# Eight weight slots from the middle of the output projections on, and the high part of x ahead of its square

## The chip, the core and the metric

The kernel runs as one program on one core of a Trainium2 chip. What is measured is the device time of one execution in microseconds (us). In the text, "PE" is TensorE, "ACT" ScalarE, "DVE" VectorE, "POOL" GpSimd and "SP" SyncE.

## The reference, cut to what matters

512 tokens of width 1024 pass through a gMLP layer, a squared-ReLU MLP, a banded attention layer, a second squared-ReLU MLP, a SwiGLU half step, a mixer with two branches (sparse attention and retention), a second SwiGLU half step and a gated addition. Every product is a float32 matrix product, and in front of most of them stands an RMS norm of the running stream h:

```python
def rms_norm(x, g):
    y = xf * lax.rsqrt(jnp.mean(xf * xf, axis=-1, keepdims=True) + RMS_EPS)
    return (y * g).astype(x.dtype)

h = h + rms_norm(m, g[1])                                      # m: output projection of the layer
f = sq_relu_mlp(rms_norm(h, g[2]), w_up[layer], w_down[layer])
h = h + rms_norm(f, g[3])
...
h = h + merged @ w_out[i]
h = h + 0.5 * swiglu(rms_norm_2(h, ffn2_norm[i]), ...)
```

## The kernel before, in words

**Split products.** PE multiplies in fp32r. Weights and activations are each split into a high and a low part, and a product is three passes per tile: high weights with high x, high weights with low x, low weights with high x. Activations are feature-major: eight tiles of 128 features by 512 tokens. XH and XL hold the two parts of x, and HH and HL those of a hidden activation.

**Units.** All weights form one list of 411 units of 128 x 1024, in the order of use. FIRST names where each product begins: gmlp_out at 16, ffn_a0 at 24, att_v at 88, att_out at 112, ffn_a1 at 120, ffn_b1 at 184, mix_heads at 252, merge at 287, mix_out at 319, ffn_b2 at 327, ple at 395. SP loads unit u into one of four raw buffers once unit u - 4 is split. Splitting is two instructions: high (a copy to fp32r) and low (raw minus high). For the units of POOL_RANGES both are done by POOL (L362, L365). For the others ACT makes the high part (split_high, L865) and DVE the low part (split_low, L1206), eight units ahead of the product whose output they are taking (AHEAD). The first such unit behind a POOL range waits until POOL has finished the range: DVE by `dve.wait_ge(weights_split, SLOTS + u)`, ACT by its counterpart on high_split.

**Slots.** Split weights lie in four slots (WH, WL) or, inside the ranges of WIDE, in eight (WH2, WL2 and, where these are taken, WHA and WLA). A slot may be filled when the unit before it in that slot is done (`units_done`). With four slots that is unit u - 4, with eight it is u - 8. WIDE begins one or two groups behind each output projection.

**PE's products.** `product` takes one unit, and a plain unit is 24 matmuls. `together` takes three or four units side by side, feature tile by feature tile, so that it can begin while later tiles of x are still being made. `token_major_half` does the same with x as the stationary operand. Before the last tile they call `stat`, which sums the squares over the partitions and must wait for the last of them; afterwards `spread` lays 1/rms out over the partitions. The bank of PSUM for a unit is u mod 4, but a few units (SPARE) use bank 7.

**A norm.** x is scaled by 1/rms only after the product, so the parts of x need the gain alone. For each tile t, DVE updates H, ACT writes the square to T (`square`) and the high part to XH, and DVE adds the square to SS (`add_square`) and writes XL (`pre_tile`). `post_and_pre` is the norm behind an MLP or projection whose own output was normed, `half_step` that behind a SwiGLU. `branch` evacuates an output projection tile by tile: DVE copies the bank, ACT squares it, DVE adds the square, and then DVE's split_low for eight units ahead stands in the same queue.

Of the kernel before, what the change touches and what calls it, by code (L numbers as in the profile page):

```python
# [151 lines left out]
def program(nc, xT, weights, gains, cols, lng, lnb, bs, wsT, rel, pos, ident_d, decay, pT, out):  # L152
    with ExitStack() as ctx:
# [32 lines left out]
        WHA = at("WHA", 188, [P, 3, UNIT], F32R)  # L186
# [156 lines left out]
        def _(pool):  # L343
# [3 lines left out]
            def split_units(u, n, step=0):  # L347

                for v in range(u, u + n):
# [40 lines left out]
        def _(pe):  # L390
# [4 lines left out]
            ss, ri = Count(ss_ready), Count(ri_ready)  # L395
# [40 lines left out]
            def together(*units, before_last=None):  # L436


# [31 lines left out]
            def token_major_half(ready=None, before_last=None):  # L470


                first = split.n
                for q in range(4):
# [4 lines left out]
                    for kk in range(2):  # L479
# [3 lines left out]
                        if ready is not None:  # L483
                            pe.wait_ge(ready.sem, ready.now(back=DT - 1 - k))
                        w = slice(kk * SEQ, kk * SEQ + SEQ)
                        for j in range(TT):
                            tok = slice(j * P, j * P + P)
                            for n, (x, wt) in enumerate(((XH, high), (XL, high), (XH, low))):
                                last = nc.tensor.matmul(PS[:, (first + j) % SLOTS, :], x[:, k, tok],  # L489
                                                        wt[:, w], start=(k == 0 and n == 0),  # L490
                                                        stop=(k == DT - 1 and n == 2))
                    last.then_inc(units_done, 1)

            def products_token_major(ready=None, before_last=None):

                if ready is not None:
                    token_major_half(ready, before_last)
# [30 lines left out]
            def ffn(tiles, gated):  # L528
# [3 lines left out]
                def group(size, first=False):  # L532
                    if first:
                        together(*[(DT, XH, XL, xr)] * SLOTS, before_last=stat)
                        spread(5)
# [73 lines left out]
            products_token_major(xr, stat)  # L609
# [14 lines left out]

            xr.next(DT)
# [4 lines left out]
            products_token_major(xr, stat)  # L630
# [19 lines left out]
            def out_high(n, k):  # L650

                w = slice(k * P, k * P + P)
                nc.tensor.matmul(PS[:, out_bank(n), :], WH[:, n % SLOTS, w], OH[:, k, :], start=(k == 0), stop=False)
                return nc.tensor.matmul(PS[:, out_bank(n), :], WL[:, n % SLOTS, w], OH[:, k, :], start=False,
                                        stop=False)

            def out_low(n, k):
# [3 lines left out]
                                        WH[:, n % SLOTS, w], OL[:, :, w], start=False, stop=(k == DT - 1))  # L661
# [85 lines left out]

            xr.next(DT)
            ffn(FFN_A, False)
            stat_and_spread()  # L750

            xr.next(DT)
# [3 lines left out]
            together(*[(DT, XH, XL, xr)] * 3, before_last=stat)  # L756
# [64 lines left out]

            xr.next(DT)
# [14 lines left out]
        def _(act):  # L837
# [983 lines left out]
```

## Time and profile before

| | |
|---|---|
| device time, median of 3 runs | 2685.99 us (2682.25 to 2686.25) |
| the profiled execution's own time | 2688.23 us |
| its span in the trace | 2686.4 us |
| granted clock of PE, mean of the span | 0.944 |
| PE busy | 2489.5 us (93%) |
| DVE, ACT, POOL busy | 1364.6, 760.4, 610.2 us |

Times inside the trace count from the start of the span. The granted clock is 1.0 when PE runs at 2.4 GHz and 0.5 at 1.2 GHz. A busy share is an average over stages, and what ends last in each stage is read from the waits and the timeline.

### The profile page before, as it was taken

The numbers are of one execution on the slowest core, as the hardware profiler recorded it, in microseconds if no ns is written. First come the engines' busy times: TensorE is split into PE (matmuls) and PEld (weight loads), VectorE is DVE, ScalarE is ACT, GpSimd is POOL, SyncE is SP. The second block draws the span as 40 slices with busy tenths as digits, with TensorE's granted clock in tenths as the row PEclk, the third lists the DMA queues.
The fourth block names the chain that finished last, engine by engine and source line by source line (L and its number), as shares of the span: only waits on it lengthen the run. The fifth ranks groups of instructions, "written<-read, shape, count | busy, mean of one in ns | idle before, by whom it ended". The sixth has DMA issues, their size and how long they took to land.

```text
span 2686.4 us, 29675 instructions
## 1 busy us (share of the span) xinstructions
PE 2489.5 (93%) x10924; PEld 1980.5 (74%) x10924; DVE 1364.6 (51%) x1947; ACT 760.4 (28%) x1200; POOL 610.2 (23%) x283
## 2 busy tenths in 40 slices
PE   6878999989996999998999997978899997999997
PEld 5666888877665788887888885664478885888886
DVE  4546434463663643445564456796344344544465
ACT  2114323331432432233322233302322111322232
POOL 6650000025335000000000005551037875000000
PEclk9888999989998999998999998985599998999999
DMA  4222333322223233331332322120012332433321
GB/s 166 73 78 68 110 97 99 94 63 77 78 63 94 63 102 102 94 99 55 118 101 87 92 81 63 55 71 24 16 40 78 94 94 79 117 97 92 93 77 59
DMA packets 64823, 221.79 MB, mean 83 GB/s; under 512 B 7504, under 2 KB 9680, under 8 KB 64592
## 3 DMA queue, kind: packets, MB, share of 16 engines
q1 hardware_dynamic: 59184, 208.17, 26.2%
q10 hardware_dynamic: 5536, 12.19, 1.4%
q8 instruction: 72, 1.18, 0.2%
q14 instruction: 31, 0.25, 0.0%
HBM read 218.23 MB, written 2.10 MB: 82 GB/s over the span
## 4 chain that ended last, share of the span: by engine, by line
PE 80%; DVE 10%; POOL 4%; ACT 3%; issue 2%; DMA 0%; POOLq 0%; ACTq 0%; DVEq 0%
PE PS L420 23%; PE PS L422 22%; PE PS L421 22%; PE PS L489 3%; POOL WH L362 2%; POOL WL L365 2%; PE PS L563 1%; PE PS L584 1%; DVE WL L1206 1%; PE PS L774 1%; PE PS L690 1%; PE PS L711 1%; PE PS L700 1%; DVE MK L1574 1%; PE PS L573 1%
## 5 line engine op out<-in xcount | busy, mean ns | idle before, releaser
L420 PE MATMUL PS<-XH,WH 128*128 128x512 f32 x1792 | 714.6, 399 | 40.2 <-DVE T L1425 12.5
L421 PE MATMUL PS<-XL,WH 128*128 128x512 f32 x1792 | 703.7, 393 | 0.0
L422 PE MATMUL PS<-XH,WL 128*128 128x512 f32 x1784 | 700.4, 393 | 0.0
L362 POOL TENSOR_TENSOR WH<-RAW,ONES 128x1024 fp32r<-128x1024 f32 (+1 forms) x136 | 266.9, 1963 | 1654.8 <-PE PS L422 1530.3
L1206 DVE TENSOR_TENSOR WL<-RAW,WH 128x1024 fp32r<-128x1024 f32 (+2 forms) x272 | 322.4, 1185 | 248.4 <-ACT WH L865 192.2
L420 PEld LDWEIGHTS PS<-XH,WH 128*128 128x128 f32 x1792 | 340.8, 190 | 130.7 <-issue 33.6
L422 PEld LDWEIGHTS PS<-XH,WL 128*128 128x128 f32 x1784 | 338.5, 190 | 72.0
L420 PE MATMUL PS<-HH,WH 128*128 128x512 f32 x992 | 389.0, 392 | 2.6 <-DVE HL L1278 2.6
L421 PEld LDWEIGHTS PS<-XL,WH 128*128 128x128 f32 x1792 | 340.6, 190 | 68.2
L422 PE MATMUL PS<-HH,WL 128*128 128x512 f32 x992 | 386.3, 389 | 0.0
L421 PE MATMUL PS<-HL,WH 128*128 128x512 f32 x992 | 386.1, 389 | 0.0
L865 ACT ACTIVATE WH<-RAW 128x1024 fp32r<-128x1024 f32 (+2 forms) x272 | 276.8, 1018 | 349.5 <-DVE M L1309 202.4
L365 POOL TENSOR_TENSOR WL<-RAW,WH 128x1024 fp32r<-128x1024 f32 (+1 forms) x132 | 322.5, 2443 | 10.4
L420 PEld LDWEIGHTS PS<-HH,WH 128*128 128x128 f32 x992 | 186.2, 188 | 50.0 <-issue 9.1
L422 PEld LDWEIGHTS PS<-HH,WL 128*128 128x128 f32 x992 | 186.2, 188 | 38.9
L421 PEld LDWEIGHTS PS<-HL,WH 128*128 128x128 f32 x992 | 186.3, 188 | 37.9
L1278 DVE TENSOR_TENSOR HL<-T,HH 128x512 fp32r<-128x512 f32 x108 | 74.8, 692 | 127.2 <-ACT HH L928 92.7
L489 PE MATMUL PS<-WH,XH 128*128 128x512 f32 x192 | 82.3, 428 | 46.4 <-DVE XL L1226 22.4
L1218 DVE TENSOR_TENSOR SS<-SS,T 128x512 f32<-128x512 f32 x91 | 82.8, 910 | 24.5 <-ACT T L871 24.5
L925 ACT ACTIVATE T<-T 128x512 f32<-128x512 f32 x64 | 40.5, 632 | 184.9 <-DVE T L1285 184.9
L1309 DVE TENSOR_TENSOR M<-PS,M 128x512 f32<-128x512 f32 x48 | 33.1, 690 | 107.2 <-PE PS L422 106.8
L871 ACT ACTIVATE T<-H 128x512 f32<-128x512 f32 x72 | 45.4, 631 | 141.5 <-DVE H L1255 48.4
(208 smaller groups left out, 2467.6 us busy)
## 6 DMA issues: line engine op xcount, KB each, us to landing
RAW<-in_weights SPq DMA_DIRECT2D x379, 512.0 KB, 3.5
RAW<-in_weights SPq DMA_DIRECT2D x16, 384.0 KB, 3.2
H<-in_xT ACTq DMA_DIRECT2D x8, 256.0 KB, 8.2
BIAS<-in_rel ACTq DMA_DIRECT2D x8, 256.0 KB, 3.5
RAW<-in_weights SPq DMA_DIRECT2D x8, 256.0 KB, 2.7
out<-R ACTq DMA_DIRECT2D x8, 256.0 KB, 2.2
BIAS<-in_rel ACTq DMA_DIRECT2D x8, 224.0 KB, 3.9
DECAY<-in_decay ACTq DMA_DIRECT2D x1, 1024.0 KB, 4.9
```

Source lines behind the costliest of these rows:

```text
L362: nc.gpsimd.tensor_tensor(high[:, 0:w], raw, ONES[:, 0:1].to_broadcast([P, w]), ALU.mult).then_inc(high_split, 1)
L365: nc.gpsimd.tensor_tensor(low[:, 0:w], raw, high[:, 0:w].bitcast(F32), ALU.subtract).then_inc(weights_split, 1)
L420: nc.tensor.matmul(PS[:, bank_, :], high[:, w], xh[:, k, :], start=(k == 0), stop=False)
L421: nc.tensor.matmul(PS[:, bank_, :], high[:, w], xl[:, k, :], start=False, stop=False)
L422: return nc.tensor.matmul(PS[:, bank_, :], low[:, w], xh[:, k, :], start=False, stop=stop)
L489: last = nc.tensor.matmul(PS[:, (first + j) % SLOTS, :], x[:, k, tok], wt[:, w], start=(k == 0 and n == 0), stop=(k == DT - 1 and n == 2))
L865: S.activation(weights_of(u)[0][:, 0:w], RAW[:, slot, 0:w], ACT.Copy).then_inc(high_split, 1)
L871: S.activation(T[:, sq.n % 2, :], src, ACT.Square).then_inc(sq_ready, 1)
L925: S.activation(T[:, 1, :], T[:, 0, :], ACT.Square).then_inc(act_self, 1)
L1206: V.tensor_tensor(low[:, 0:w], RAW[:, slot, 0:w], high[:, 0:w].bitcast(F32), ALU.subtract).then_inc(weights_split, 1)
L1218: V.tensor_tensor(SS[:], SS[:], T[:, slot, :], ALU.add).then_inc(ss_ready, 1)
L1278: V.tensor_tensor(HL[:, f, :], T[:, src, :], HH[:, f, :].bitcast(F32), ALU.subtract).then_inc(h_ready, 1)
```

## The change

Two independent edits are made.

First, WIDE begins four units earlier: at 20, 116 and 323, the middle of the three output projections. POOL's splits of these units wait for other conditions (all low parts of x made, all scores read, all units before mix_out done) and not for the unit four places back. Free memory for the slots is taken from other places (WHX, WLX), and WHA goes away. The third POOL range ends at 331 instead of 335, so ACT and DVE split units 331 to 334.

Second, in the norms ACT writes the high part before the square, DVE writes XL before it adds the square (`low_part`, then `square_and_rest`), and in `post_and_pre` and `half_step` the low part of tile t - 1 stands between the two instructions that update H of tile t. In the first product of a norm PE waits for the high part alone (xh_ready), runs the two passes that read XH, then waits for XL and runs the third pass. This form is used for the first product of the first norm, of ffn_a0, att_v, ffn_a1, ffn_b1, mix_heads and ffn_b2. The first products of gmlp_out, mix_out and ple stay as they were.

```diff
-POOL_RANGES = ((0, 28), (92, 124), (256, 335))
+POOL_RANGES = ((0, 28), (92, 124), (256, 331))
-WIDE = ((24, 92, 20), (120, 256, 116), (331, UNITS, 328))
+WIDE = ((20, 92, 16), (116, 256, 112), (323, UNITS, 319))
...
-        WHA = at("WHA", 188, [P, 3, UNIT], F32R)
+        WHX = [at(f"WHX{n}", kb, [P, UNIT], F32R) for n, kb in enumerate((72, 76, 88, 92))]
+        WLX = [at(f"WLX{n}", kb, [P, UNIT], F32R) for n, kb in enumerate((188, 92, 192, 196))]
...
-            high = WHA[:, k - SLOTS, :] if 331 < u < 335 else WH2[:, k - SLOTS, :]
-            low = WLA[:, k - SLOTS, :] if 120 <= u < 124 else WL2[:, k - SLOTS, :]
+            high = WHX[k - SLOTS] if 323 <= u < 335 else WH2[:, k - SLOTS, :]
+            low = WLA[:, 2 * SLOTS - 1 - k, :] if 116 <= u < 120 else WLX[k - SLOTS] if 124 <= u < 128 else                 WL2[:, k - SLOTS, :]
...
-                    if v == 24:
+                    if v == FIRST["gmlp_out"] + SLOTS:
                         pool.wait_ge(x_ready, 2 * DT)
-                    elif v == 120:
+                    elif v == FIRST["att_out"] + SLOTS:
                         pool.wait_ge(x_done, 2 * DT * TT)
-                    elif v == 332:
+                    elif v == FIRST["mix_out"] + SLOTS:
                         pool.wait_ge(units_done, FIRST["mix_out"] + SLOTS)
...
+                    if high:
+                        pe.wait_ge(xh_ready, high(k))
+                        w = slice(k * P, k * P + P)
+                        for s, (tiles, xh, xl, ready) in enumerate(units):
+                            if k == 0:
+                                pe.wait_ge(weights_split, split.next())
+                                pe.wait_ge(evacuated, bank.next())
+                            for n, part in enumerate(weights_of(first + s)):
+                                nc.tensor.matmul(PS[:, (first + s) % SLOTS, :], part[:, w], xh[:, k, :],
+                                                 start=(k == 0 and n == 0), stop=False)
+                        pe.wait_ge(ready.sem, ready.now(back=tiles - 1 - k))
+                        for s, (tiles, xh, xl, ready) in enumerate(units):
+                            last = nc.tensor.matmul(PS[:, (first + s) % SLOTS, :], weights_of(first + s)[0][:, w],
+                                                    xl[:, k, :], start=False, stop=(k == tiles - 1))
+                            if k == tiles - 1:
+                                last.then_inc(units_done, 1)
+                        continue
...
             def pre_norm(gs, free, ready, evacuates=None):
+                act.wait_ge(units_done, free + SLOTS)
                 for t in range(DT):
                     act.wait_ge(ready.sem, ready.next())
-                    square(H[:, t, :])
-                    if t == 0:
-                        act.wait_ge(units_done, free + SLOTS)
-                    for g, dst in gs:
+                    for n, (g, dst) in enumerate(gs):
                         S.activation(dst[:, t, :], H[:, t, :], ACT.Copy, scale=gain(g, t)).then_inc(xh_ready, 1)
+                        if n == 0:
+                            square(H[:, t, :])
...
+            def low_part(t, g, dh, dl, ready):
+                dve.wait_ge(xh_ready, xh.next())
+                V.scalar_tensor_tensor(dl[:, t, :], H[:, t, :], gain(g, t), dh[:, t, :].bitcast(F32),
+                                       ALU.mult, ALU.subtract).then_inc(ready, 1)
+
+            def square_and_rest(t, gs):
+                add_square(t == 0)
+                for g in gs[1:]:
+                    low_part(t, *g)
+
             def pre_tile(t, gs):
-                add_square(t == 0)
-                for g, dh, dl, ready in gs:
-                    dve.wait_ge(xh_ready, xh.next())
-                    V.scalar_tensor_tensor(dl[:, t, :], H[:, t, :], gain(g, t), dh[:, t, :].bitcast(F32),
-                                           ALU.mult, ALU.subtract).then_inc(ready, 1)
+                low_part(t, *gs[0])
+                square_and_rest(t, gs)
```

## Rows read from the trace of the kernel before

**Rows 1.** The page: busy time, share of the span and instructions of each engine.

```profile
PE 2489.5 (93%) x10924; PEld 1980.5 (74%) x10924; DVE 1364.6 (51%) x1947; ACT 760.4 (28%) x1200; POOL 610.2 (23%) x283
```

**Rows 2.** The waits of PE: who waited for whom, total us, times, longest.

```profile
PE PS L509 <- DVE SS L1218: 45.1, 5, 19.0
...
PE PS L420 <- POOL WL L365: 9.8, 4, 4.1
PE PS L420 <- DVE T L1297: 9.1, 1, 9.1
```

**Rows 3.** Stretches A:B, their length, each engine's busy time, clock, DMA share, GB/s.

```profile
161.00:189.50 28.50, 28.50 (x127) 23.45 (x125) 9.02 (x10) 3.17 (x5) 27.81 (x13) 1.00 0.30 93
189.50:207.80 18.30, 0.20 (x1) 0.00 (x0) 7.55 (x9) 5.68 (x7) 7.85 (x4) 0.56 0.53 152
847.50:866.40 18.90, 0.00 (x0) 0.00 (x0) 7.53 (x9) 5.61 (x7) 8.52 (x5) 0.58 0.51 147
...
2226.00:2238.00 12.00, 3.69 (x12) 1.90 (x10) 12.00 (x6) 2.52 (x3) 11.74 (x5) 0.79 0.29 87
...
2269.40:2278.40 9.00, 0.08 (x1) 0.00 (x0) 1.81 (x2) 1.06 (x1) 6.99 (x4) 0.75 0.40 120
```

**Rows 4.** Timeline of POOL, gmlp_out: first and last of sixteen (start, us, line, out<-in).

```profile
161.22 1.89 POOL L362 TENSOR_TENSOR WH<-RAW,ONES 128x1024 fp32r<-128x1024 f32 x1 [23.62 <-PE PS L422]
...
195.16 2.35 POOL L365 TENSOR_TENSOR WL<-RAW,WH 128x1024 fp32r<-128x1024 f32 x1
```

**Rows 5.** Timeline of DVE, around gmlp_out.

```profile
151.17 1.47 DVE L1438 TENSOR_TENSOR XL<-T,XH 128x512 fp32r<-128x512 f32 x2
...
197.54 1.22 DVE L1206 TENSOR_TENSOR WL<-RAW,WH 128x1024 fp32r<-128x1024 f32 x1 [21.45 <-POOL WL L365]
```

**Rows 6.** Timelines of DVE and of POOL, around att_out.

```profile
809.13 0.69 DVE L1491 CUSTOM_DVE_ANT_0 PROB<-PS,BIAS 128x512 f32<-128x512 f32 x1
...
856.21 1.22 DVE L1206 TENSOR_TENSOR WL<-RAW,WH 128x1024 fp32r<-128x1024 f32 x1 [21.45 <-POOL WLA L365]
```
```profile
819.89 1.89 POOL L362 TENSOR_TENSOR WH<-RAW,ONES 128x1024 fp32r<-128x1024 f32 x1 [25.52 <-PE PS L660]
```

**Rows 7.** Timelines of POOL and of DVE, around mix_out and the start of ffn_b2.

```profile
2184.89 2.72 POOL L365 TENSOR_TENSOR WL<-RAW,WH 128x1024 fp32r<-128x1024 f32 x1
2197.87 1.89 POOL L362 TENSOR_TENSOR WH<-RAW,ONES 128x1024 fp32r<-128x1024 f32 x1 [10.26 <-PE PS L422]
...
2235.23 2.67 POOL L365 TENSOR_TENSOR WL<-RAW,WH 128x1024 fp32r<-128x1024 f32 x1
2259.38 1.89 POOL L362 TENSOR_TENSOR WH<-RAW,ONES 128x1024 fp32r<-128x1024 f32 x1 [21.48 <-PE PS L422]
```
```profile
2205.08 2.88 DVE L1226 SCALAR_TENSOR_TENSOR XL<-H,GAIN,XH 128x512 fp32r<-128x512 f32 x1
...
2276.59 1.22 DVE L1206 TENSOR_TENSOR WL<-RAW,WH 128x1024 fp32r<-128x1024 f32 x1 [12.92 <-POOL WL L365]
```

**Rows 8.** Timelines of ACT, PE and DVE, start of the norm of ffn_a1; PE's clock.

```profile
872.60 0.63 ACT L871 ACTIVATE T<-H 128x512 f32<-128x512 f32 x1 [3.96 <-DVE H L1255]
```
```profile
875.09 0.77 PE L420 MATMUL PS<-XH,WH 128*128 128x512 f32 x1 [4.11 <-DVE XL L1226]
```
```profile
876.85 0.74 DVE L1226 SCALAR_TENSOR_TENSOR XL<-H,GAIN,XH 128x512 fp32r<-128x512 f32 x1
...
879.49 0.75 DVE L1226 SCALAR_TENSOR_TENSOR XL<-H,GAIN,XH 128x512 fp32r<-128x512 f32 x1
```
```profile
872.50:881.20 8.70, 6.11 (x14) 4.79 (x15) 8.56 (x15) 4.97 (x8) 0.00 (x0) 0.50 0.01 2
```

**Rows 9.** The first norm: timelines of POOL and DVE, and one stretch.

```profile
32.75 3.00 POOL L362 TENSOR_TENSOR WH<-RAW,ONES 128x1024 fp32r<-128x1024 f32 x1 [3.70 <-PE PS L489]
```
```profile
33.91 2.38 DVE L1226 SCALAR_TENSOR_TENSOR XL<-H,GAIN,XH 128x512 fp32r<-128x512 f32 x1
```
```profile
35.00:40.00 5.00, 5.00 (x24) 4.14 (x23) 1.29 (x1) 0.00 (x0) 4.92 (x3) 1.00 0.14 19
```

More of the change, by code:

```diff
@@ L434, in piece, with together @@
                     last.then_inc(units_done, 1)
-            def together(*units, before_last=None):
+            def together(*units, before_last=None, high=None):
                 first = split.n - SLOTS
@@ L482, in token_major_half, with products_token_major @@
                             before_last()
-                        if ready is not None:
-                            pe.wait_ge(ready.sem, ready.now(back=DT - 1 - k))
                         w = slice(kk * SEQ, kk * SEQ + SEQ)
[L486 to L491, printed above, removed]
+                        if high_now:
+                            pe.wait_ge(xh_ready, high_now(k))
+                        for passes in ((XH, high), (XH, low)), ((XL, high),):
+                            if ready is not None and passes[0][0] is XL:
+                                pe.wait_ge(ready.sem, ready.now(back=DT - 1 - k))
+                            for j in range(TT):
+                                tok = slice(j * P, j * P + P)
+                                for x, wt in passes:
+                                    last = nc.tensor.matmul(PS[:, (first + j) % SLOTS, :], x[:, k, tok], wt[:, w],
+                                                            start=(k == 0 and x is XH and wt is high),
+                                                            stop=(k == DT - 1 and x is XL))
                     last.then_inc(units_done, 1)
-            def products_token_major(ready=None, before_last=None):
+            def products_token_major(ready=None, before_last=None, high_now=None):
                 if ready is not None:
-                    token_major_half(ready, before_last)
+                    token_major_half(ready, before_last, high_now)
                     spread(5)
@@ L533, in group @@
                     if first:
-                        together(*[(DT, XH, XL, xr)] * SLOTS, before_last=stat)
+                        together(*[(DT, XH, XL, xr)] * SLOTS, before_last=stat, high=lambda k: xp.now() + k + 1)
                         spread(5)
@@ L608, in _ @@
             xr.next(DT)
-            products_token_major(xr, stat)
+            products_token_major(xr, stat, lambda k: k + 1)
             products(XH, XL)
@@ L629, in _ @@
             xr.next(DT)
-            products_token_major(xr, stat)
+            xp.n = 3 * DT
+            products_token_major(xr, stat, lambda k: xp.now() + 2 * k + 1)
             pe.wait_ge(h_ready, hr.next(DT))
@@ L755, in _ @@
             xr.next(DT)
-            together(*[(DT, XH, XL, xr)] * 3, before_last=stat)
+            xp.n = 7 * DT
+            together(*[(DT, XH, XL, xr)] * 3, before_last=stat, high=lambda k: xp.now() + k + 1)
             spread(5)
@@ L995, in _ @@
                 act.wait_ge(in_x[t], 16)
+                S.activation(XH[:, t, :], H[:, t, :], ACT.Copy, scale=gain(G_MIX0, t)).then_inc(xh_ready, 1)
                 square(H[:, t, :])
-                S.activation(XH[:, t, :], H[:, t, :], ACT.Copy, scale=gain(G_MIX0, t)).then_inc(xh_ready, 1)
             norm_rows()
@@ L1253, in post_and_pre @@
                         z = T[:, 2 + t % 2, :]
-                        link(V.tensor_tensor(z, m[:, t, :], PS[:, 4, :], ALU.mult))
+                        V.tensor_tensor(z, m[:, t, :], PS[:, 4, :], ALU.mult).then_inc(dve_self, 1)
+                        me.next()
+                    if t:
+                        low_part(t - 1, *gs[0])
+                    if t < DT:
+                        dve.wait_ge(dve_self, me.now())
                         V.scalar_tensor_tensor(H[:, t, :], z, gain(g_out, t), H[:, t, :],
```

23 lines of the change are left out of this document (15 added, 8 removed).

## The prediction, on record before the result

> **What bounds the kernel now.** I read the page first. PE is busy for 93% of the span [rows 1], so only what lies between its stretches can be saved: 2686.4 - 2489.5 = 197 us of idle, plus time at half clock. Next the waits of PE. The largest group, 45.1 us in five waits, is `stat` waiting for the last sum of squares, the longest 19.0; then come 9.8 us for POOL's low weight parts in four waits and a single 9.1 us for a DVE evacuation (L1297) [rows 2]. The stretches place them: PE does nothing from 189.5 to 207.8 and from 847.5 to 866.4, works for 3.69 of 12 us at 2226 to 2238 and stops again from 2269.4 to 2278.4 [rows 3]. These are the ends of gmlp_out and att_out, the handover from mix_out to ffn_b2, and the first plain unit of ffn_b2.
>
> The timelines say why. In gmlp_out POOL splits units 20 to 27 in one chain of sixteen instructions. It starts at 161.22 when unit 16 is done and ends at 195.16 + 2.35 = 197.5 [rows 4]. DVE's evacuation queue holds the low split of unit 28 between two evacuations, and this waits for POOL's range: DVE is idle for 21.45 us until 197.54 and only then takes the last three banks [rows 5]. PE finished its products at 189.5. So the path is POOL, then DVE's tail of 207.8 - 197.5 = 10.3 us, then `stat`. att_out repeats it: POOL starts at 819.89, DVE is released at 856.21 after the same 21.45 us [rows 6], and `stat` runs at 866.4.
>
> **First edit, output projections.** In gmlp_out the new condition for unit 20 is that all XL of the gate are made, at 151.17 + 1.47 = 152.6 [rows 5]. POOL's eight units take 36.3 us (161.2 to 197.5). They wait for nothing else: unit 24 needs unit 16, done at 161.2, and POOL reaches it near 170. So the chain ends at 152.7 + 36.3 = 189.0 and the tail of 10.3 gives `stat` at 199.3 instead of 207.8: **8.5 us**. PE's own end at 189.5 is before DVE needs the last bank, so it doesn't bound.
>
> In att_out the condition for unit 116 is the last score read, 809.13 + 0.69 = 809.8 [rows 6]. POOL would end 10.1 us earlier at the same pace. But it now runs beside the last softmax of the attention, and there DVE and POOL hinder each other. The clearest row is XL: 2.88 us while POOL splits [rows 7] against 0.74 when it rests [rows 8]. POOL loses too: eight units take 2197.87 to 2237.9, 40.0 us, where DVE issues two such instructions per unit [rows 7], and 36.3 us where it issues about four in all [rows 4]. That is (40.0 - 36.3) / 12 = 0.3 us per meeting, at most 0.45. I expect three or four more meetings, 1.5 us: **8.5 us** for att_out, bounds 7.5 and 10. DVE's last softmax steps come up to 2 us later each, which moves PE's end from 847.5 to perhaps 850. The last bank isn't taken before 855, so that is hidden.
>
> The Trainium skill ("SBUF — State Buffer", section "Who interferes with whom") has a rule that speaks against moving POOL's work here: whichever of the two starts first holds the shared ports for its whole instruction and the other is fully blocked. By this rule a meeting costs POOL a whole DVE instruction, and att_out would keep 1 to 1.5 us less than by the rows. DVE's 2.88 us agrees with full blocking.
>
> **First edit, mix_out.** POOL ended the split of unit 322 at 2184.89 + 2.72 = 2187.6 and then stood 10.26 us until units 319 to 321 were done [rows 7]. The new condition (all units before 319 done) is met by then. So POOL runs on: two units unhindered at some 4.35 us, six at 40.0 / 8 = 5.0, end at 2187.6 + 8.7 + 30 = 2226.3. But this wait has a successor. In the loop over tiles DVE now has the low splits of 331 to 334, and the first must wait for POOL's unit 330. Behind it stand H(6) and H(7), which free two of the four banks that PE's next `together` needs. From 2226.5: split 1.2, H(6) 0.7, XL 0.7, add 0.6, split 1.2, H(7) 0.7, together 5.1 us. PE gets its fourth bank at about 2232 where it got its fourth weights at 2237.9 (rows 3: PE nearly idle to 2238): **5.9 us**. PE's own products end near 2226 in both.
>
> After `together` POOL split units 331 to 334 in one more chain from 2259.38, and DVE's evacuation of the second bank waited behind the split of 335, released at 2276.59 after 12.92 us [rows 7]. With these splits done earlier by ACT and DVE both waits go: the 9.1 us of rows 2, and the fourth of the four waits on POOL (three lie before 2238). That one is 9.8 less the 8.3 us PE stood idle in the 12 us stretch [rows 3], **1.5 us**. The next evacuation is then due when PE finishes unit 331, so the whole **9.1 us** is saved within half a microsecond.
>
> **Second edit, norms.** Take ffn_a1. H(0) is there at 872.6 and ACT spends 0.63 us on the square first [rows 8]. PE starts at 875.09, released by XL(0). Now ACT writes XH first (0.7 us), so PE starts at 873.35, 1.74 us earlier. Is XL late then? It comes at about 874.1, while PE's eight matmuls on XH take 8 x 0.43 = 3.4 us: at half clock 14 matmuls ran in the 6.1 us from 875.1 to 881.2 [rows 8]. At full clock they come every 28.5 / 127 = 0.225 us [rows 3], twelve in 2.7 us. DVE needs 879.49 - 876.85 = 2.64 us per tile [rows 8], so PE stays the slower one and keeps its lead to the end. `stat` before the last tile needs the last square, which now comes after XL(7), and PE arrives later than both. ffn_a0 and ffn_b1 have the same form: 3 x 1.7 = **5.1 us**, bounds 3.5 and 6, since the clock rises some microseconds after the start and this can shift by one or two either way. In att_v DVE makes a second low part per tile, 3.3 us in all, and PE runs into it. The end then hangs on the last square, which moves little: **1 us**, bounds 0 and 1.7. In the first product of mix_heads and of ffn_b2 PE has seven tiles of work (14 us and more) ahead of the last tile, so the order there costs and gives nothing. Matmuls and their number are unchanged, as are DVE's and ACT's.
>
> The first norm is the uncertain one. POOL splits the first units through it, so DVE's instructions take 2.38 us and more [rows 9]. XL now stands before the add, some 2.3 us earlier, so PE finishes unit 1 up to 4 us earlier. But this releases POOL's split of unit 5 directly behind unit 4, where POOL had been idle for 3.70 us [rows 9] and DVE made up four tiles at 1.3 us each. DVE then stays hindered to the end and its last add, for which `stat` waits, may come about 3 us later than `stat` did. Before, DVE was done by 36.3 with PE busy beyond 40 [rows 9], so some of this is covered. Bounds: 4.4 us gained, 3 us lost. I take **2 us lost**, because the mutual release seems to me the likelier course.
>
> **The sum.** 8.5 + 8.5 + 5.9 + 1.5 + 9.1 + 5.1 + 1.0 - 2.0 = 37.6 us. The profiled execution took 2688.2, its span 2686.4, and the median of the runs is 2686.0. I subtract from the median: 2648.4, so 2648.
>
> **Rivals.**
> - The successor wait in mix_out eats its 5.9 us (POOL's chain slower than 5.0 per unit, DVE stopped until 2232): 2654. For it speaks that DVE and ACT both now stand behind POOL; against it that POOL starts 10 us sooner. Chance 0.12.
> - The first norm goes the good way, 4 us gained instead of 2 lost: 2642. It depends on whether DVE is through before POOL gets its next unit. Chance 0.13.
> - DVE and POOL meet far more often than I counted, and the meetings cost att_out 4 us, mix_out 3 and the first norm 2 more: 2657. Chance 0.10.
> - POOL's start isn't what frees PE, something in DVE's queue is, and nothing moves: 2686. The 21.45 us idle row speaks against. Chance 0.03.
> - Slower: waiting twice per tile keeps PE's clock at its lower level through the norms' first products. 96 matmuls at 0.43 instead of 0.225 are 19.7 us, of which 14 matmuls (2.9 us) are slow already, so 16.8 us for each. From three such stretches on it outweighs the 37.6; with four of the seven it gives 2716. Against it: the second wait of a tile is short or nothing. Chance 0.02.
>
> The forecast itself has 0.60, with 2642 to 2655 as its own range. From the single bounds the total gain is between 29 and 47 us, so the range is 2639 to 2657. A measurement of this kernel can tell about 0.2%, 5.4 us, from no change. Faster 0.95, same 0.03, slower 0.02.
>
> **What would show it.** Right: POOL's chain of eight units starts right behind the last XL of the gate, the last score and unit 322; DVE's idle time at the low splits of units 28 and 124 shrinks from 21.45 to about 13; PE's idle stretch before `stat` is some 10 us in both projections; no wait of 9 us on L1297; PE starts each norm less than 1 us after ACT has H(0), where it was 2.5; in mix_out, with 21 us of the sum lying before it, DVE's H(7) comes near 2232 - 21 = 2211. Wrong: POOL's chain longer than 38 us beside the softmax, a new long wait of PE for DVE's H(7), a `stat` in the first norm later than 40.7, or the clock at half through more than the first 6 us of a norm.

## The result and the profile after

| | before | after |
|---|---|---|
| device time, median of 20 runs each | 2682.89 us | 2690.11 us |
| lowest and highest | 2676.33, 2720.92 us | 2683.12, 2691.66 us |
| span of the profiled execution | 2686.4 us | 2688.6 us |
| granted clock of PE, mean of the span | 0.944 | 0.935 |

The ratio is 1.0022, with an interval of 1.0015 to 1.003: slower by 0.2%, where 2648 was forecast. The page shows PE busy for 38 us longer with the same 10924 matmuls [rows 1]:

```profile
PE 2527.7 (94%) x10924; PEld 1994.4 (74%) x10924; DVE 1376.0 (51%) x1951; ACT 764.9 (28%) x1204; POOL 591.6 (22%) x275
...
PEclk8898999989998999999999996587589999999999
```

```profile
PEclk9888999989998999998999998985599998999999
```

The last line of each is PE's clock in 40 slices of 67 us (after first, then before). Slices 25 and 26, from 1613 to 1748 us, show 6 and 5 after, 8 and 9 before; the low place some 200 us behind is in both. To find all changes, I compared the start of each matmul in the two traces, counted from PE's first one (14.47 us before, 11.22 after; a value of this table less 3.25 is the difference on the traces' own clocks). The matmuls are the same in number, and almost in order, so the running difference tells where time is won and lost. It compares one execution with one other.

| behind | after minus before | change | forecast |
|---|---|---|---|
| first norm | +6.5 | +3.3 on the traces' own clocks | +2.0 |
| gmlp_out and the norm of ffn_a0 | -3.8 | -10.3 | -8.5 - 1.7 |
| first product of att_v | +6.0 | +9.8 | -1.0 |
| att_out and the norm of ffn_a1 | -6.2 | -12.3 | -8.5 - 1.7 |
| norm of ffn_b1 | -10.0 | -3.8 | -1.7 |
| matmul at which PE starts again after the wait in mix_heads | -15.8 | -5.8 | 0 |
| the index stage of mix_heads | +26.2 | **+42.0** | 0 |
| rest of the mixer | +24.7 | -1.5 | 0 |
| mix_out and the first units of ffn_b2 | +4.6 | -20.1 | -16.5 |

Nearly all that was forecast is there, some with interest, and two entries against it: 9.8 us in att_v and 42.0 at what I call the index stage. There `product` for units 259 to 262 runs, and behind each tile's three matmuls stands one small matmul of the index scores (the trace holds two records for each of these, 64 in all). By the stretches (columns as in [rows 3]), first of the kernel before, then after:

```profile
1645.20:1659.10 13.90, 0.00 (x0) 0.00 (x0) 12.35 (x10) 5.01 (x8) 10.68 (x5) 0.64 0.38 113
1659.10:1713.00 53.90, 53.88 (x164) 26.50 (x164) 34.11 (x49) 22.78 (x47) 13.77 (x7) 0.97 0.10 30
```

```profile
1632.30:1640.00 7.70, 0.00 (x0) 0.00 (x0) 7.13 (x7) 2.51 (x4) 4.57 (x2) 0.69 0.46 135
1640.00:1734.30 94.30, 94.25 (x164) 43.30 (x164) 33.41 (x49) 23.31 (x47) 14.06 (x7) 0.50 0.06 17
190.60:202.50 11.90, 0.19 (x1) 0.00 (x0) 7.56 (x9) 4.87 (x7) 1.64 (x1) 0.68 0.53 155
852.20:859.50 7.30, 0.00 (x0) 0.00 (x0) 5.40 (x7) 3.52 (x5) 0.00 (x0) 0.83 0.59 168
2224.00:2236.00 12.00, 12.00 (x55) 9.94 (x54) 12.00 (x9) 2.49 (x4) 11.77 (x6) 1.00 0.41 127
```

The same 164 matmuls take 53.9 us before and 94.3 after, PE is busy throughout in both, and the clock is 0.97 in one and 0.50 (1.2 GHz) in the other. So this loss is no wait: 40.4 us here, and 1.6 right behind the stage, until the clock rises. In both kernels PE stands idle directly ahead of the stage and starts again when DVE has written T: 14.4 us from matmul to matmul before, 8.2 after. The groups by line show it on a single operation, the index matmuls (before, then after, with 482 and 815 ns each on average over their four shapes):

```profile
L774 PE MATMUL PS<-IK,AQIQ 64*128 64x256 f32 (+3 forms) x60 | 24.1, 482 | 0.0
```

```profile
L797 PE MATMUL PS<-IK,AQIQ 64*128 64x128 f32 (+3 forms) x63 | 45.0, 815 | 0.0
```

The other stretches of after are what the forecast asked for. PE is idle for 11.9 us ahead of `stat` in gmlp_out, where it was 18.3 [rows 3], and for 7.3 in att_out (18.9), and it no longer pauses in mix_out's last 12 us (it worked for 3.69 of them).

### The profile page after: what moved, and what is told of

Same layout as the page of the kernel before. It is cut to its first block, busy times and chain, and to the rows that moved or that the text cites. A ratio compares the mean times of both kernels' runs of the same rounds, so it can differ in the third digit from the quotient of the medians.

```text
span 2688.6 us, 29599 instructions
## 1 busy us (share of the span) xinstructions
PE 2527.7 (94%) x10924; PEld 1994.4 (74%) x10924; DVE 1376.0 (51%) x1951; ACT 764.9 (28%) x1204; POOL 591.6 (22%) x275
## 4 chain that ended last, share of the span: by engine, by line
PE 79%; DVE 11%; POOL 4%; ACT 3%; issue 2%; DMA 0%; POOLq 0%; ACTq 0%; DVEq 0%
PE PS L421 21%; PE PS L423 21%; PE PS L422 21%; PE PS L507 3%; PE PS L452 2%; POOL WL L366 2%; POOL WH L363 2%; PE PS L797 2%; PE PS L581 1%; PE PS L602 1%; PE PS L456 1%; DVE SS L1242 1%; PE PS L710 1%; DVE WL L1230 1%; PE PS L731 1%
## 5 line engine op out<-in xcount | busy, mean ns | idle before, releaser
L421 PE MATMUL PS<-XH,WH 128*128 128x512 f32 x1632 | 655.4, 402 | 18.1 <-DVE T L1466 12.5
L423 PE MATMUL PS<-XH,WL 128*128 128x512 f32 x1632 | 644.8, 395 | 0.0
L422 PE MATMUL PS<-XL,WH 128*128 128x512 f32 x1632 | 644.7, 395 | 0.0
L363 POOL TENSOR_TENSOR WH<-RAW,ONES 128x1024 fp32r<-128x1024 f32 (+1 forms) x131 | 254.7, 1944 | 1645.1 <-DVE WL L1230 734.3
L421 PEld LDWEIGHTS PS<-XH,WH 128*128 128x128 f32 x1632 | 310.7, 190 | 112.5 <-issue 34.8
L423 PEld LDWEIGHTS PS<-XH,WL 128*128 128x128 f32 x1632 | 311.9, 191 | 66.6
L422 PEld LDWEIGHTS PS<-XL,WH 128*128 128x128 f32 x1632 | 312.2, 191 | 61.0
L366 POOL TENSOR_TENSOR WL<-RAW,WH 128x1024 fp32r<-128x1024 f32 (+1 forms) x127 | 310.4, 2444 | 10.0
L422 PEld LDWEIGHTS PS<-HL,WH 128*128 128x128 f32 x992 | 186.4, 188 | 37.6
L507 PE MATMUL PS<-WH,XH 128*128 128x512 f32 x192 | 83.9, 437 | 40.4 <-DVE T L1564 13.9
L507 PE MATMUL PS<-WL,XH 128*128 128x512 f32 x192 | 82.4, 429 | 0.0
```

Source lines behind the costliest of these rows:

```text
L363: nc.gpsimd.tensor_tensor(high[:, 0:w], raw, ONES[:, 0:1].to_broadcast([P, w]), ALU.mult).then_inc(high_split, 1)
L366: nc.gpsimd.tensor_tensor(low[:, 0:w], raw, high[:, 0:w].bitcast(F32), ALU.subtract).then_inc(weights_split, 1)
L421: nc.tensor.matmul(PS[:, bank_, :], high[:, w], xh[:, k, :], start=(k == 0), stop=False)
L422: nc.tensor.matmul(PS[:, bank_, :], high[:, w], xl[:, k, :], start=False, stop=False)
L423: return nc.tensor.matmul(PS[:, bank_, :], low[:, w], xh[:, k, :], start=False, stop=stop)
```

## The experiments

Ratios are to the kernel before on the same chip, with a 95% interval. "After" is the changed kernel. Where microseconds are given against after, its 2690.11 comes from another set of runs; the medians of the kernel before in the four sets lie between 2682.3 and 2683.9 us, so this adds up to 1.6 us of doubt. Each expectation says what the theories that it names would give. B (PE's new order in the norms keeps the clock low) fell with e1_slots and e2_norms, C (the shorter pause does) with e5_late256. D (the moment at which PE restarts decides) is what e9 to e12 bear out, against its rival E.

**e1_slots and e2_norms: each edit alone.** In the one the norms stay as before; in the other slots and ranges do.

> The first edit alone (weight slots and POOL's ranges). Theory A, read from the two traces: the projections gain (8 us in gmlp_out, 12 in att_out with its norm, 20 in mix_out and ffn_b2), att_v loses up to 10 us because the ring of eight slots is shifted by four and units 92 to 95 now wait for units 88 to 91, so that POOL splits inside the norm. The index stage of mix_heads (products of eight units interleaved with index scores, 1640 to 1737 in the changed kernel) runs at half clock or not, depending only on when it starts: ratio 0.988 if its clock rises, 1.00 if it stays low. Rival B: the norms' new order keeps the clock low in the index stage; then this kernel must have it high and be near 0.988. Rival C: the slots' part in the index stage does it (unit 256 now waits for 248 instead of 252); then it is low here.

> The second edit alone (order in the norms, high part first on PE). Theory A: the first norm loses 3 us against its absolute time (POOL's split of unit 5 is released into DVE's last tiles), ffn_a0, ffn_a1 and ffn_b1 gain 1.7 us or more each, att_v gains 1 us because POOL has already split units 92 to 95 by then. Sum about -3 us, ratio 0.999, and 1.012 if the index stage happens to fall into half clock. Rival B (the norms' order keeps the index stage slow): 1.012 for certain. Rival C: 0.999 for certain.

Measured: the slots alone 2691.09 us (1.0022, 1.0012 to 1.0031), the norms alone 2685.37 (1.0003, 0.9987 to 1.0019). With the slots alone the index stage runs at half clock from end to end, as in after; with the norms alone the clock came back 9.3 us after the restart:

```profile
1646.40:1740.70 94.30, 94.30 (x164) 43.22 (x164) 33.44 (x49) 23.33 (x47) 14.18 (x7) 0.50 0.06 17
```

```profile
1646.00:1655.30 9.30, 9.22 (x22) 5.57 (x22) 4.57 (x10) 3.23 (x7) 0.00 (x0) 0.50 0.01 4
1655.30:1702.70 47.40, 47.40 (x144) 22.26 (x144) 29.57 (x40) 19.56 (x41) 14.12 (x7) 1.00 0.12 34
```

So PE's order in the norms doesn't hold the clock down, and the loss in att_v belongs to the slots: e1_slots loses 7.8 us there and 1.6 more close behind, while e2_norms gains 2.2. (The expectation speaks of eight units in the index stage; they are four, 259 to 262.)

**e3_warm: PE kept at work ahead of the index stage.** 32 matmuls of no use, into a bank that nobody reads, fill the wait.

```diff
             product(DT, XH, XL)
+            for _ in range(32):
+                nc.tensor.matmul(PS[:, 6, :], XH[:, 0, 0:P], XH[:, 0, :], start=True, stop=True)
             pe.wait_ge(evacuated, v_ready)
```

> The changed kernel with 32 more matmuls of XH with itself into an unused bank, behind the product in front of the index stage, where PE otherwise waits 7.8 us for DVE. They compute nothing that is used. Theory A: PE keeps full clock into the index stage, which then takes some 65 us instead of 100: 34 to 36 us less than the changed kernel, ratio to before 0.989, and the granted clock of the stretch is 1.0. Rival B or C with another mechanism than the clock's start (too few columns in the stage itself): the clock falls back within the stage and at most 5 us are gained, ratio 1.000.

Measured: 2645.78 us (0.9857, 0.9835 to 0.9879), 44.3 us less than after. The stage starts and stays at full clock:

```profile
1636.80:1689.70 52.90, 52.55 (x164) 25.36 (x164) 34.10 (x49) 22.68 (x47) 13.97 (x7) 1.00 0.11 31
```

The same 164 matmuls take 52.6 us at this level and 94.3 at the other, 41.7 us less, so the clock is the whole of the large loss. The expectation had put this at 34 to 36 us and the gain was 44.3.

**e4_hold: POOL kept out of two norms.** It waits for all squares before it splits unit 5, and again before unit 92.

```diff
...
+                    if v in (5, 92):
+                        pool.wait_ge(ss_ready, DT if v == 5 else 5 * DT)
```

> The changed kernel with one more wait on POOL in front of units 5 and 92: the sum of squares of the norm in progress must be complete (ss_ready at 8 and at 40). So POOL splits nothing while DVE makes the last tiles of the first norm and any tile of att_v's. Theory A: the first norm gains 3 to 6 us and att_v some 10 us against the changed kernel; the index stage may change its state, since it starts elsewhere. Ratio to before 0.997 with the index stage slow, 0.984 with it fast. Rival: POOL's splits in the norms are covered and the loss is the double waiting of PE; then nothing is gained and PE waits for POOL's unit 92 afterwards, 1.002 to 1.004.

Measured: 2671.84 us (0.9956, 0.9939 to 0.9973), 18.3 less than after. The running difference is -9.42 ahead of att_v and -9.65 behind it, so att_v's 9.8 us are won back. The first norm gives 5.8 more in this pair of executions (+0.7 instead of +6.5); how much such a figure varies is said under "First norm" below, but the medians, 18.3 us apart, leave 8.5 for it too. In after POOL's splits of the range begin in att_v's norm (L363 and L366 for each unit), where before it had split unit 95 by 573.88 + 2.67 = 576.6 and then rested for 44.90 us:

```profile
573.88 2.67 POOL L365 TENSOR_TENSOR WL<-RAW,WH 128x1024 fp32r<-128x1024 f32 x1
621.45 1.89 POOL L362 TENSOR_TENSOR WH<-RAW,ONES 128x1024 fp32r<-128x1024 f32 x1 [44.90 <-PE PS L489]
```

```profile
581.27 2.52 POOL L363 TENSOR_TENSOR WH<-RAW,ONES 128x1024 fp32r<-128x1024 f32 x1 [389.03 <-PE PS L507]
...
588.46 2.35 POOL L363 TENSOR_TENSOR WH<-RAW,ONES 128x1024 fp32r<-128x1024 f32 x1 [1.89 <-PE PS L507]
...
600.51 2.35 POOL L363 TENSOR_TENSOR WH<-RAW,ONES 128x1024 fp32r<-128x1024 f32 x1 [6.93 <-PE PS L507]
```

The timeline of DVE in after shows what this does to DVE: an instruction of 0.75 us alone takes 2.3 to 2.8 when it meets POOL.

```profile
578.16 0.68 DVE L1242 TENSOR_TENSOR SS<-SS,T 128x512 f32<-128x512 f32 x1
578.76 0.74 DVE L1248 SCALAR_TENSOR_TENSOR HL<-H,GAIN,HH 128x512 fp32r<-128x512 f32 x1
...
581.95 2.38 DVE L1248 SCALAR_TENSOR_TENSOR HL<-H,GAIN,HH 128x512 fp32r<-128x512 f32 x1
584.26 0.67 DVE L1287 TENSOR_TENSOR T<-M,PS 128x512 f32<-128x512 f32 x1
584.86 2.27 DVE L1248 SCALAR_TENSOR_TENSOR XL<-H,GAIN,XH 128x512 fp32r<-128x512 f32 x1
...
601.03 2.38 DVE L1248 SCALAR_TENSOR_TENSOR HL<-H,GAIN,HH 128x512 fp32r<-128x512 f32 x1
603.34 2.82 DVE L1248 SCALAR_TENSOR_TENSOR XL<-H,GAIN,XH 128x512 fp32r<-128x512 f32 x1
606.08 0.68 DVE L1242 TENSOR_TENSOR SS<-SS,T 128x512 f32<-128x512 f32 x1
```

The norm has seven adds to SS. Before, they started between 584.8 and 603.3, within 18.5 us. In after the first is at 578.16 and the last, for which `stat` waits, at 606.08: 27.9 us. In e4_hold it is 17.8 (572.0 to 589.8). PE's clock over the product is 0.79 in after, 0.82 before and 0.87 in e4_hold. The index stage is unchanged at half clock (91.5 us from its first to its last index matmul), so the two losses are separate.

**e5_late256: POOL's second early chain.** At unit 256 the shifted ring of slots lets POOL begin a half step earlier too, and this is why the idle time ahead of the index stage is 8.2 us in after. Theory C was that this shorter pause, with POOL's splits where they now stand, keeps the clock down.

```diff
+                    if 256 <= v < 260:
+                        pool.wait_ge(units_done, v - SLOTS + 1 + SLOTS)
```

> The changed kernel with one thing of the old ring of slots put back: POOL splits units 256 to 259 only when units 252 to 255 are done (before the change the slots themselves asked for that; now they ask for 248 to 251). POOL then works beside DVE's rotations in mix_heads again, and PE's idle time in front of the index stage grows from 8.2 us to the 14.4 us it had before. Theory C: whether PE's clock comes back at the start of the index stage hangs on that idle time and what goes with it, so this kernel has it at full level as the kernel before: 34 us less than the changed kernel minus some 2 us for the longer wait, ratio 0.989. Rival D: it hangs on the moment of the restart alone, which every edit ahead moves; then the clock stays at half (ratio 1.004) or differs from run to run by 36 us.

Measured: 2695.35 us (1.0042, 1.0029 to 1.0054). The pause is back at its 14.4 us (1634.0 to 1648.4), but the full clock is not:

```profile
1634.20:1648.40 14.20, 0.18 (x1) 0.00 (x0) 12.66 (x10) 5.02 (x8) 10.98 (x5) 0.59 0.38 110
1648.40:1742.70 94.30, 94.28 (x164) 43.27 (x164) 33.44 (x49) 23.33 (x47) 14.11 (x7) 0.50 0.06 17
```

So the length of the pause alone doesn't decide it, and theory C fell.

**e6_burst: twelve matmuls at the restart.** They stand behind the wait, so the pause remains and only what PE does first is changed.

```diff
             pe.wait_ge(evacuated, v_ready)
+            for _ in range(12):
+                nc.tensor.matmul(PS[:, 6, :], XH[:, 0, 0:P], XH[:, 0, :], start=True, stop=True)
```

> The changed kernel with 12 more matmuls of XH with itself into an unused bank (unused result) at the restart itself, behind PE's wait for DVE in front of the index stage. The idle time of 8.2 us and the fall of the clock stay as they are. If the interleaved stage can't raise the clock by itself but keeps it once it is up, these 12 raise it: they cost 12 x 0.43 = 5 us or less and save 34 to 36, ratio 0.990. If the clock falls back in the stage, ratio 1.004.

Measured: 2648.99 us (0.9873, 0.9856 to 0.9889), 41.1 less than after, though the burst itself takes 5.44 us. The clock is low from 1627.1 for 10.2 us and full from the end of the burst on. So the mix of three large matmuls and a small one keeps the clock up once it is up, but in after, e1_slots, e4_hold and e5_late256 it didn't bring it back.

**e7_warm_hold: both remedies.**

> The changed kernel with both repairs, the 32 extra matmuls ahead of the index stage (results unused) and POOL's wait in front of units 5 and 92. The two lie in different stages and should add: 2690 - 44 - 18 = 2628 us, ratio 0.979. If they overlap, as when the first only moved the phase of the second, it is nearer to 2640 (0.984).

Measured: 2630.26 us (0.9803, 0.9786 to 0.9819), the fastest version here, 52.6 us less than before. Alone the remedies gave 44.3 and 18.3 us against after; 2690.1 - 62.6 = 2627.5, so they add up within 3 us.

**e8_before_warm: the 32 matmuls in the kernel before.**

> The kernel before with the same 32 extra matmuls (results unused) ahead of the index stage and nothing of the change. Its idle time there is 14.4 us, so the 32 end 7 us before the restart and the clock falls all the same. In most executions the stage came back to full clock by itself, so the median stays within 3 us of the kernel before, ratio 1.000. If the extra matmuls are what gave the changed kernel its gain by other means than the clock of this stage, it is faster here too, by 10 us or more (0.996 or less).

Measured: 2684.97 us (1.0023, 0.999 to 1.0057), no gain. The kernel before mostly had the clock back without help, and here the 32 end 6.8 us ahead of the restart, so they don't fill the pause. Three of its ten runs were at 2721 to 2722, and so was one of the 20 runs of before (2720.92), and two of e2's ten (2722, 2726). These lie some 38 us above the rest, about what the stage at half clock costs. Their granted clock over the whole execution speaks for the same stage: 0.932 or 0.933 in e8's three, where its other seven have 0.947 or more, and 0.929 to 0.931 in e12_before_shift8 below, whose profiled run has the stage at half clock. It isn't shown, since none of them is the profiled run.

**e9_shift4, e10_shift8, e11_shift12 and e12_before_shift8: nothing but the timing.** 4, 8 or 12 extra matmuls at the end of ffn_b1, far ahead of the pause, put 0.9, 1.8 or 2.7 us (4, 8 or 12 x 0.228) ahead of all that follows and change nothing in it. The last of the four puts 8 of them into the kernel before.

```diff
             ffn(FFN_B, True)
+            for _ in range(8):
+                nc.tensor.matmul(PS[:, 6, :], HH[:, 0, 0:P], HH[:, 0, :], start=True, stop=True)
```

> The changed kernel with 4 more matmuls of HH with itself into an unused bank (result unused) at the end of ffn_b1, in a stretch where PE never waits. They move everything behind them, the restart in front of the index stage too, by 4 x 0.227 = 0.9 us, and change neither the idle time of 8.2 us nor the order of anything. Theory D (the level at which the clock stays in the index stage hangs on the moment of the restart, which any edit moves): for some of the three moves of 0.9, 1.8 and 2.7 us the clock comes back and the kernel takes 2654 us, ratio 0.989. Theory E (it hangs on what POOL, DVE and the slots do in the stage since the first edit): none of the three comes back, ratio 1.003.

> As the one with 4, with 8 more matmuls: a move of 1.8 us. Theory D: this is about the farthest from where the changed kernel restarts, so the clock should come back here if anywhere, 2655 us and ratio 0.990. Theory E: 2692 us, ratio 1.003.

> As the one with 4, with 12 more matmuls: a move of 2.7 us. Theory D: it comes back or not, with executions of both kinds possible, some 36 us apart; ratio 0.990 or 1.003. Theory E: 2693 us, ratio 1.004.

> The kernel before with 8 more matmuls (result unused) at the end of ffn_b1: a move of 1.8 us. Theory D: the kernel before owes its full clock in the index stage to the moment of its restart, so with this move more executions stay at half clock: at least a third of them near 2720 us. Theory E: all but a few are near 2685 us, ratio 1.001.

| kernel | shift | median us | ratio (95%) | index stage, profiled run |
|---|---|---|---|---|
| after | 0 | 2690.11 | 1.0022 (1.0015 to 1.003) | 91.5 us, half clock |
| e9_shift4 | 0.9 us | 2654.68 | 0.9903 (0.9872 to 0.9934) | 91.5, half; runs at both levels |
| e10_shift8 | 1.8 us | 2649.78 | 0.9881 (0.9859 to 0.9903) | 51.4, full |
| e11_shift12 | 2.7 us | 2691.45 | 1.0031 (1.0017 to 1.0045) | 91.5, half |
| before | 0 | 2682.66 | 1 | 51.3, full but for the start |
| e12_before_shift8 | 1.8 us | 2728.16 | 1.0175 (1.0155 to 1.0194) | 91.5, half |

e9's ten runs fall in two groups, seven at 2645 to 2659 with a granted clock of 0.949 to 0.955 and three at 2684 to 2690 with 0.937 to 0.939. The stretches of e10_shift8 and e12_before_shift8 are the clearest pair of the study. The first is the changed kernel with more work and 40 us less in all of its four runs, the second the kernel before with the same more work and 45 us more in all of its four:

```profile
1632.90:1640.90 8.00, 0.20 (x1) 0.00 (x0) 7.40 (x7) 2.51 (x4) 4.57 (x2) 0.82 0.45 130
1640.90:1695.10 54.20, 54.18 (x164) 26.58 (x164) 34.11 (x49) 22.77 (x47) 13.97 (x7) 0.96 0.10 30
```

```profile
1642.20:1656.10 13.90, 0.00 (x0) 0.00 (x0) 12.37 (x10) 5.02 (x8) 10.70 (x5) 0.57 0.38 112
1656.10:1750.50 94.40, 94.36 (x164) 43.25 (x164) 33.41 (x49) 23.33 (x47) 14.20 (x7) 0.50 0.06 17
```

And e11_shift12, the changed kernel with 12 of them:

```profile
1634.50:1642.30 7.80, 0.01 (x1) 0.01 (x1) 7.17 (x7) 2.51 (x4) 4.57 (x2) 0.76 0.44 133
1642.30:1736.60 94.30, 94.30 (x164) 43.23 (x164) 33.45 (x49) 23.31 (x47) 14.13 (x7) 0.50 0.06 17
```

In e10_shift8 PE waits for the same instruction as in after, for the same time (7.82 against 7.81 us), and restarts with the same work. Only the timing differs, and 8 more full-rate matmuls among hundreds at the end of ffn_b1. e11_shift12 has still more of these and is slow again in all its eight runs, so more of them doesn't mean a better clock. That a change of timing alone decides whether the clock comes back in this stage is thereby shown, in both kernels; theory E fell.

Which moment counts is not shown, but it can't be the time since the start. The profiled executions differ upstream by more than the shifts: the restart is at 1640.05 us in after, 1635.7 in e9, 1640.9 in e10 and 1642.3 in e11, at 1659.1 before and 1656.1 in e12. What does order them is how long the clock had been low when PE restarted, by the clock of the pause's row (2 x (1 - clock) x length; after: 2 x 0.31 x 7.7 = 4.8 us). With the pause of 7.8 us it is 2.9 us in e10 (full clock), 3.7 in e11, 4.8 in after and e1_slots, 5.0 in e4_hold and 5.4 in e9 (all half). With the pause of 14 us it is 10.0 in before (full 3.8 us after the restart), 11.1 in e2_norms (full 9.3 us after it), 11.6 in e5_late256 and 12.0 in e12 (both half). In each group the earlier restart behind the clock's fall has the full clock. This is an order among single executions, seen afterwards; no run varied it alone, and what the chip's control looks at is open.

## Why the prediction was wrong

**What failed** first is a term that the sum doesn't have. It is in the paragraph on the second edit: "Matmuls and their number are unchanged, as are DVE's and ACT's", taken as if the price of each were unchanged too. I gave mix_heads neither a gain nor a loss. In its place the runs showed 5.8 us won in the pause of mix_heads and 42.0 lost in the index stage. The rival on the clock had the right mechanism in the wrong place: I looked for it in the norms' first products, where the edit changes PE's order, and gave it 0.02. It came in a stage whose work neither edit touches. The edits change its timing, and e9 to e12 show that this is enough. The index stage costs 40.2 us more between its first and last index matmul (91.5 - 51.3). Without these the profiled run would have taken 2688.6 - 40.2 = 2648.4, the forecast number, but this agreement is partly luck. att_v's 9.8 us lost stand against gains above the forecast (5.8 in the pause, 3.6 around mix_out, 2.1 in ffn_b1). The base was off too: I subtracted from 2686.0, the median of three runs, and the median of twenty is 2682.9. e10_shift8 less its 1.8 us of extra work, 2648.0, is 34.7 us below the kernel before beside it (2682.66), where 37.6 was forecast. The second step that failed is att_v, below.

The Trainium skill ("TensorE: Matmul & The Clock Gate", Part 1) says that for modelling the penalty of the clock's ramp is under 1% of a typical kernel's span. This is said of the ramp behind a start. The trace shows something that such a figure doesn't cover: a stage that never leaves half clock, and costs 40.2 of 2688.6 us, 1.5%, by itself.

**gmlp_out, 8.5 forecast.** `stat` is at 202.55 (207.8 before), 5.3 us earlier, though PE came into the product 2.4 us later (first matmul at 146.99 instead of 144.58): 7.7 us gained. POOL's chain is released by the last XL and takes 36.2 us, DVE's idle time is 15.24 instead of 21.45:

```profile
156.00 1.89 POOL L363 TENSOR_TENSOR WH<-RAW,ONES 128x1024 fp32r<-128x1024 f32 x1 [15.18 <-DVE XL L1479]
...
189.87 2.37 POOL L366 TENSOR_TENSOR WL<-RAW,WH 128x1024 fp32r<-128x1024 f32 x1
```

```profile
154.38 1.48 DVE L1479 TENSOR_TENSOR XL<-T,XH 128x512 fp32r<-128x512 f32 x2
...
192.27 1.23 DVE L1230 TENSOR_TENSOR WL<-RAW,WH 128x1024 fp32r<-128x1024 f32 x1 [15.24 <-POOL WL L366]
```

**att_out, 8.5 forecast.** 866.5 to 859.6, with PE 2.8 us later on the way in: 9.7 us. POOL's chain beside the softmax takes 812.76 to 849.27, 36.5 us. I had added 1.5 us for more meetings with DVE than in gmlp_out, and they cost 0.2, so the rival with many meetings fell for this place. A meeting shows as 2.35 us at 830.36 where POOL alone takes 1.89, 0.46 more. The Trainium skill ("SBUF — State Buffer", "Who interferes with whom") has the later of the two fully blocked; by it I had put the chain 1 to 1.5 us longer still, and the trace shows it shorter. On DVE's side (0.75 against at most 2.8 us in att_v, where POOL's instruction takes 2.35) the rule and the trace agree.

```profile
812.76 1.90 POOL L363 TENSOR_TENSOR WH<-RAW,ONES 128x1024 fp32r<-128x1024 f32 x1 [15.61 <-DVE NMX L1532]
...
830.36 2.35 POOL L363 TENSOR_TENSOR WH<-RAW,ONES 128x1024 fp32r<-128x1024 f32 x1
...
846.87 2.40 POOL L366 TENSOR_TENSOR WL<-RAW,WH 128x1024 fp32r<-128x1024 f32 x1
```

**mix_out and ffn_b2, 16.5 forecast, 20.1 measured.** The chain of units 323 to 330 runs from 2209.13 to 2247.90, 38.8 us as forecast (8.7 + 30), and the successor wait is there and short. The mixer ends 21.5 us later than before on the traces' own clocks, so H(7) at 2252.08 + 0.69 = 2252.8 stands for 2231.3, where the forecast had 2232 (in absolute time it had 2211, since it knew nothing of the index stage and att_v). The handover gave 24.7 - 18.0 = 6.7 us against 5.9, the plain units behind it 13.4 against 10.6, among other things since the clock no longer falls to 0.75 there [rows 3].

```profile
2247.94 1.23 DVE L1230 TENSOR_TENSOR WL<-RAW,WHX 128x1024 fp32r<-128x1024 f32 x1 [2.31 <-POOL WL L366]
...
2250.94 1.22 DVE L1230 TENSOR_TENSOR WL<-RAW,WHX 128x1024 fp32r<-128x1024 f32 x1
2252.08 0.69 DVE L1697 TENSOR_TENSOR H<-PS,H 128x512 f32<-128x512 f32 x1
```

The 9.1 us wait of PE for the evacuation in ffn_b2 is gone. By the waits of PE from 2240 to 2300 us only those for H(6) and H(7) are left there:

```profile
PE PS L452 <- DVE H L1697: 3.5, 2, 2.3
```

Of the whole span these rows bear on the forecast: `stat`, whose longest wait is now 11.8 us (19.0 before [rows 2]), and the three norm starts, 2.5 at most:

```profile
PE PS L527 <- DVE SS L1242: 33.0, 7, 11.8
...
PE PS L452 <- ACT XH L905: 7.4, 3, 2.5
```

**Norms, 1.7 each forecast.** In ffn_a1 DVE has H(0) at 864.92 + 0.75 = 865.67 and PE starts 0.9 us later, where it was 2.5:

```profile
864.92 0.75 DVE L1293 SCALAR_TENSOR_TENSOR H<-T,GAIN,H 128x512 f32<-128x512 f32 x1
...
865.76 0.72 ACT L905 ACTIVATE XH<-H,GAIN 128x512 fp32r<-128x512 f32 x1 [4.02 <-DVE H L1293]
...
866.54 0.80 PE L452 MATMUL PS<-XH,WH 128*128 128x512 f32 x1 [2.45 <-ACT XH L905]
```

ffn_a0 gave 1.8 us and ffn_a1 2.6. ffn_b1 gave 3.8: the mechanism held, the size was low by 2.1. The rest of that I didn't trace.

**First norm, 2 lost forecast, 3.3 lost.** `stat` is at 42.48 instead of 40.7; the rest follows in the matmuls behind it, some of them at half clock (0.63 us instead of 0.40). The mutual release came as described: POOL had only 2.54 us of rest (3.70 before [rows 9]) until PE released its next unit, and DVE's last two instructions take 2.38 and 2.82 us. But 3.3 us is the figure of one execution, and it doesn't hold for the kernel. By the same count, the profiled executions of the other versions with this first norm unchanged from after are at +1.4 (e3), +4.9 (e5), -3.4 (e6), -1.7 (e9), +2.9 (e10), +3.2 (e11) and, with the norms alone, -0.6 (e2). The kernel before repeats within 0.2 (e8, e12). So this norm goes either way from one execution to the next, and both the loss and the rival of a gain occurred; I didn't trace what decides. With POOL held back `stat` is at 37.64 (e4_hold) instead of 42.48, and the profiled executions of e4 and e7 are at -3.1 and -5.2 by the same count, so this norm can gain.

```profile
36.83 2.29 POOL L363 TENSOR_TENSOR WH<-RAW,ONES 128x1024 fp32r<-128x1024 f32 x1 [2.54 <-PE PS L507]
```

```profile
36.69 0.68 DVE L1242 TENSOR_TENSOR SS<-SS,T 128x512 f32<-128x512 f32 x1
37.30 2.38 DVE L1248 SCALAR_TENSOR_TENSOR XL<-H,GAIN,XH 128x512 fp32r<-128x512 f32 x1
39.60 2.82 DVE L1242 TENSOR_TENSOR SS<-SS,T 128x512 f32<-128x512 f32 x1
```

**att_v, 1 gained forecast, 9.8 lost.** This step failed too, and for a reason that stands in the diff. The loss is steady: the profiled executions of after, e3, e5, e6, e9, e10 and e11 all lose 8.7 to 9.8 us here. Units 92 to 95 stand behind the wide range, in the four plain slots, and each waits for the last unit in its slot. With WIDE's last number, the zero of the ring, at 16 instead of 20, these are units 88 to 91, the first half of att_v itself, where they had been 84 to 87, done before the norm. I had read the shift at its near end, units 20 to 27, and not at the far end of the same range. At 256 the same shift works the other way, to an earlier owner (248 instead of 252), and there it brings some 6 us less idle time ahead of the index stage.

**Which of the things to look for.** Right: the chains' starts, the shorter idle time of DVE (15.24 and 10.94 us, about 13 forecast), the waits ahead of `stat` (11.8 and 7.4, about 10 forecast), no 9 us wait for an evacuation in ffn_b2, the norms' starts, and H(7) once the 21.5 us by which the mixer ends later are taken off. The warning that came true in the profiled run: `stat` of the first norm later than 40.7. The one for the clock named "a norm" and would have missed it.

## What to carry to other kernels

Where PE restarts from a pause into a stage of mixed matmuls, as here, the stage may run at either clock level, and an edit far upstream of a microsecond or two can change the time by 40 us in either direction. Compare the granted clock of each stretch before a change's own mechanism is credited or blamed. Compare several profiled executions too, since a stage such as the first norm here can differ by 8 us between two of them. Then put a short run of full-size matmuls at the restart (e6) or fill the pause (e3) before other edits are measured. The filling must reach the restart: in e8 it left 6.8 us of idle time, and three of ten runs were 38 us slower. When a ring of slots is shifted, list the earlier owner of each slot at both ends of the range.

## What the runs showed of the hardware

- A stage in which PE is busy by every record can stay at 1.2 GHz from end to end (91.5 us from the first to the last index matmul, clock 0.50), while the same instructions elsewhere have it back after 6.8 us of low clock in all (e10_shift8) or 13.7 (before). Twelve matmuls of 128x512 at the restart, 5.44 us, were enough to bring it back in e6_burst.
- POOL's chain of sixteen instructions took 36.5 us beside the softmax and 36.2 in gmlp_out. In att_v the same kind of meeting stretched single DVE instructions from 0.75 to 2.8 us, and POOL's splits there cost 9.8 us in all. The clock in that stretch is 0.79 in after and 0.87 with POOL held back, so a part of the loss may be the clock's; the runs don't separate it.
